# Expert steps of a mixture-of-experts trunk on one core: the down projection set directly ahead of the next up projection, the first scatter moved ahead of the gather, and the token tiles stored in the order in which they are loaded as weights

## The chip, the cores and the metric

The kernel runs on one core of a Trainium2 chip. Its time is the device time of one execution in microseconds (us); lower is better. A run gives a median over several executions. The profiled execution is one more, and its trace shows every instruction of every engine.

## The reference, cut to what matters

Two decoder layers over 256 tokens of width 1024, all in fp32. Each has an attention mixer, a layer norm, a mixture of experts, another layer norm and a gated embedding. The change lies in the mixture:

```python
s = sigmoid(xf @ router_w)                       # 64 experts, 8 groups
eidx = top_k(masked s + bias, 8)                 # 8 experts for each token
gates = s[eidx] / sum(s[eidx]) * 2.5
for each expert e, over the tokens that chose it:
    h = silu(xe @ w1[e]) * (xe @ w3[e])          # 1024 -> 256
    out[tok] += (h @ w2[e]) * gate               # 256 -> 1024
out += (silu(xf @ sw1) * (xf @ sw3)) @ sw2       # shared expert
```

## The kernel before, in words

Every expert gets 64 slots. The experts are taken in pairs: a **step** m works on two experts (128 slots), there are 32 steps in a layer, and four steps share one **octet** of eight experts. The slots' tokens aren't fetched by index; TensorE picks them with one-hot matrices that VectorE (DVE in the profile) builds.

What TensorE (PE) does in a step, in program order, with the line of the profile:

- **up** (`exp_up`, L907): 32 fp32 matmuls of 256 columns, which the trace shows as 64; the two experts use the two 64-column halves of the array (the profile's `128*64`). The tokens' slots are the weights, the expert's w1 and w3 in `ring` stream past.
- **gather** (`gather`, L877): two chunks of 128 features of the next octet's tokens, 8 fp32r matmuls of 512 columns on the whole array. x is split into `x_hi` and `x_lo`; a chunk of one of them is the weights, and the one-hot `sel` streams past. Feature chunk c is every eighth column, `part[:, t, c::8]`: neighbouring weights lie 32 bytes apart. It runs in the first 28 steps of a layer.
- **h transpose** (`h_transpose`, L917): 2 transposes of the step's hidden values; needs DVE's `gate_h` (L1673). ScalarE (ACT) copies the result to `hT`.
- **scatter 0** (`scatter`, L949): 4 fp32r matmuls that add the step before's outputs `y_hi` and `y_lo` into token tile 0, by the transposed one-hot `selT`, into PSUM banks 6 and 7.
- **down** (`exp_down`, L935): 8 fp32 matmuls of 512 columns (16 in the trace), on column halves as up is.
- **one-hot transpose** (`sel_transpose`, L889 and L892): 4 small bf16 matmuls for the next step; they write the PSUM bank that the h transpose used, so they wait for ACT's copy of it.
- **scatter 1** (L949): the same as scatter 0 for token tile 1, into the same two banks; it needs DVE to have added scatter 0 to `y_acc` (`add_y`, L1681).

DVE's step is `dve_step`: `gate_h`, in the last step of an octet the one-hots for the gather two octets ahead (`sel_build`, L1640, which waits for the octet's last gather), `add_y` for tile 0, `add_y` for tile 1, and `y_low` (L1687). ACT's step is silu, the copy of `hT`, the copy of the gathered tokens, `y_high` (L1249) and the copy of `selT`. SyncE (SP) loads weights into a ring of four experts: 4 MB of w1 and w3 for step m+2 once up of step m is done, then 2 MB of w2 once down of step m is done, each as DMAs of 1 MB. GpSimd (POOL) makes `x_lo` (L481, L482) once for each layer as soon as a tile's layer norm is written, and `x_hi` (L485) once the shared expert's up projection has read `xT`, whose memory it takes; the first gather waits for both. All orders are fixed by the code, and engines wait for each other by semaphores.

Of the kernel before, what the change touches and what calls it, by code (L numbers as in the profile page):

```python
# [6 lines left out]
ALU = mybir.AluOpType  # L7
# [6 lines left out]
P = 128  # L14
D = 1024
DC = D // P
# [94 lines left out]
def build_trunk(nc, a, out):  # L111
    with ExitStack() as ctx:
# [5 lines left out]
        def sem(name):  # L118
            if name not in sems:
                sems[name] = ctx.enter_context(nc.semaphore(name))  # L120
            return sems[name]
# [297 lines left out]
        @block.gpsimd  # L419
        def _(pool):  # L420
            pool.memset(small[:, 0:1024], 0.0).then_inc(sem("small_zero"), 1)
            pool.wait_ge(w_loaded[1], loaded[1])
            pool.dma_start(bgate[:, :], a["ev_b_gate"][0].partition_broadcast(P)).then_inc(sem("bias_loaded"), 16)
            pool.dma_start(fox_b[:, :], a["od_b_f"][0].partition_broadcast(P)).then_inc(sem("bias_loaded"), 16)
            pe_t = qkT[:, 16, 0:2 * HD]
            pool.dma_start(pe_t[0:CMP_LEN, 0:HD], a["ev_cmp_pos_k"][0]).then_inc(sem("cmp_loaded"), 16)
            pool.dma_start(pe_t[0:CMP_LEN, HD:2 * HD], a["ev_cmp_pos_v"][0]).then_inc(sem("cmp_loaded"), 16)
            pool.dma_start(cmp_w1[0:HD], a["ev_cmp_w1_k"][0].rearrange("(l d) f -> d l f", d=HD)).then_inc(sem("cmp_loaded"), 16)
            pool.dma_start(cmp_w1[HD:P], a["ev_cmp_w1_v"][0].rearrange("(l d) f -> d l f", d=HD)).then_inc(sem("cmp_loaded"), 16)
            pool.wait_ge(sem("small_zero"), 1)  # L430
            pool.dma_start(small[0:HD, 0:HD], a["ev_cmp_w2_k"][0]).then_inc(sem("cmp_loaded"), 16)
            pool.dma_start(small[0:HD, HD:2 * HD], a["ev_cmp_w2_v"][0]).then_inc(sem("cmp_loaded"), 16)
            def load_layer(L):
                if L == 0:
                    pool.wait_ge(sem("proj_mm0"), 2 * NT)
                else:

                    pool.wait_ge(sem(f"router_mm{L - 1}"), NT)
                    pool.wait_ge(sem(f"router_dve{L - 1}"), NT)
                    pool.wait_ge(sem(f"pT_tp{L - 1}"), NT)  # L440
                pool.dma_start(router_w[:, :, :], a["router_w"][L].rearrange("(p c) n -> p c n", c=DC)).then_inc(sem("layer_loaded"), 16)
                pool.dma_start(router_b[:, :], a["router_bias"][L].partition_broadcast(P)).then_inc(sem("layer_loaded"), 16)
                pool.dma_start(p_tok[:, :, :], a["p"][L, 0].rearrange("(t p) n -> p t n", p=P)).then_inc(sem("layer_loaded"), 16)
                load_rows(L, 0)

            def load_rows(L, n):

                g, b = (("ln1_g", "ln1_b"), ("ln2_g", "ln2_b"), ("ple_norm_g", "ple_norm_g"))[n]
                if 3 * L + n:

                    pool.wait_ge(sem("gb_used"), NT * (3 * L + n))
                pool.dma_start(gb_row[:, 0, :], a[g][L].partition_broadcast(P)).then_inc(sem("gb_loaded"), 16)
                pool.dma_start(gb_row[:, 1, :], a[b][L].partition_broadcast(P)).then_inc(sem("gb_loaded"), 16)

            load_layer(0)

            steps = [0]

            def step(ins):

                steps[0] += 1
                ins.then_inc(sem("pool_step"), 1)
                pool.wait_ge(sem("pool_step"), steps[0])

            pool.wait_ge(sem("const_loaded"), 16)
            for n, (src, heads, dst) in enumerate(((QB, 8, 20), (KS, 1, 28), (KW, 1, 30))):

                for t in range(NT):
                    pool.wait_ge(sem(f"proj_t{t}_0"), (4, 4, 5)[n])
                    ins = rope(pool, step, *rope_views(t, src, heads, dst), rope_tmp[:, :])  # L470
                    if t < NT - 1:
                        step(ins)
                ins.then_inc(sem("roped_nsa"), 1)
                pool.wait_ge(sem("roped_nsa"), n + 1)
            for L in range(DEPTH):
                if L:
                    load_layer(L)

                for t in range(NT):
                    pool.wait_ge(sem(f"ln1_out{L}"), t + 1)  # L480
                    step(pool.tensor_copy(x_lo[:, t, :], x_tok[:, t, :]))  # L481
                    step(pool.tensor_tensor(x_lo[:, t, :], x_tok[:, t, :], x_lo[:, t, :], ALU.subtract))  # L482
                pool.wait_ge(sem("shared_up"), NT * (L + 1))
                for t in range(NT):
                    pool.tensor_copy(x_hi[:, t, :], x_tok[:, t, :]).then_inc(sem("x_split"), 1)  # L485

                pool.wait_ge(sem("place_max"), L + 1)
                pool.partition_all_reduce(over_all, over_row, P, bass.bass_isa.ReduceOp.max).then_inc(sem("place_all"), 1)

                pool.wait_ge(sem("exp_up"), L * PAIRS + PAIRS - 4)  # L490
                load_rows(L, 1)
                load_rows(L, 2)
# [16 lines left out]
        def _(pe):  # L509
# [86 lines left out]
            for L in range(DEPTH):  # L596
# [273 lines left out]
                def gather(o, j, bank=0):  # L870

                    if j == 0:
                        pe.wait_ge(sem("sel_built"), o + (O0 + 1))
                    for c in range(2):
                        for t in range(NT):
                            for part in (x_hi, x_lo):
                                ins = pe.matmul(ps[:, bank + c, :], part[:, t, 2 * j + c::DC], sel[:, t, :],  # L877
                                                start=(t == 0 and part is x_hi), stop=(t == NT - 1 and part is x_lo))
                    ins.then_inc(sem("gathered"), 1)

# [59 lines left out]
                def scatter(m, t, par, first, bank=6):  # L940

                    if t == 0:
                        pe.wait_ge(sem("y_split"), m + (M0 + 1))
                    if bank == 6 and not (first and t == 0):

                        pe.wait_ge(sem("y_added"), 2 * m + (2 * M0 + t))
                    for half in range(2):
                        for part in (y_hi, y_lo):
                            ins = pe.matmul(ps[:, bank + half, :], selT[:, par, t * P:(t + 1) * P],  # L949
                                            part[:, half * PIECE:(half + 1) * PIECE],  # L950
                                            start=(part is y_hi), stop=(part is y_lo))
                    ins.then_inc(sem("scattered"), 1)

                def pe_step(m, o, odd, u, gather_next=True, selT_next=True, scatter_last=True, first=False):


                    par = u % 2
                    for b in range(2):
                        k = ks + 1 + 2 * par + b
                        if isinstance(m, int):  # L960
                            pe.wait_ge(w_loaded[k % RING], 32 * (m // 2) + loaded[k])
                        else:
                            pe.wait_ge(w_loaded[k % RING], 16 * (m - par) + loaded[k])
                    exp_up(m, o, odd, u, par, first and M0 == 0)
                    if gather_next:
                        pe.wait_ge(sem("xe_copied"), 4 * o + (4 * O0 + 4 + u))
                        gather(o + 1, u)
                    h_transpose(m)
                    if scatter_last:
                        scatter(m - 1, 0, 1 - par, M0 == 0 and isinstance(m, int) and m == 1)  # L970
                    exp_down(m, par, first and M0 == 0)
                    if selT_next:
                        sel_transpose(m + 1, o + 1 if u == 3 else o, (u + 1) % 4)
                    if scatter_last:
                        scatter(m - 1, 1, 1 - par, False)


                pe.wait_ge(sem("x_split"), NT * (L + 1))
# [330 lines left out]
        def _(dve):  # L1309
# [149 lines left out]
            for L in range(DEPTH):  # L1459
# [229 lines left out]

                def dve_step(m, o, u, build=True, build_bf=True, add=True):  # L1690
                    gate_h(m, u % 2)
                    if build and u == 3:
                        sel_build(o + 2)
                    if add:
                        add_y(m - 1, 0)
                        add_y(m - 1, 1)
                    y_low(m)
                    if build_bf and u == 2:
                        sel_bf_build(o + 1)
# [80 lines left out]
```

## Time and profile before

| | before |
|---|---|
| median of 3 runs (lowest, highest) | 1493.35 us (1493.33, 1494.79) |
| the profiled execution's own time | 1495.15 us |
| its span | 1493.4 us |
| PE busy | 1432.8 us, 96% |
| DVE, ACT, POOL busy | 34%, 24%, 3% |
| DMA | 461.89 MB, mean 309 GB/s |
| granted TensorE clock, mean | 0.981 |

The two stretches of expert steps are from 224 to 709 us and from 954 to 1439 us of the span. PE's busy time counts matmuls from start to end; since they are pipelined, the distance from one start to the next, and not a matmul's own duration, tells what one costs.

### The profile page before, as it was taken

How to read it: one execution, taken by the hardware profiler on the slowest of the kernel's cores; microseconds unless marked ns; L12 is line 12 of the kernel's file. 1: busy time of each engine (PE TensorE's matmuls, PEld its weight loads, DVE VectorE, ACT ScalarE, POOL GpSimd, SP SyncE). 2: the span in 40 equal slices, each digit the busy share in tenths (PEclk: the TensorE clock that was granted, in tenths of full speed). 3: DMA queues.
4: the chain of work that ended last, by engine and by line, in shares of the span. 5: the costliest groups of instructions: out<-in, count | busy, mean ns of one | idle time of the engine just before them, and what ended most of it. 6: DMA issues, size and time to landing. Idle time of an engine off the chain costs nothing.

```text
span 1493.4 us, 21684 instructions
## 1 busy us (share of the span) xinstructions
PE 1432.8 (96%) x8704; PEld 900.3 (60%) x8704; DVE 508.3 (34%) x840; ACT 356.5 (24%) x878; POOL 50.2 (3%) x75
## 2 busy tenths in 40 slices
PE   8978999999999999999899999999999999999988
PEld 3467586566565656654478476765666656565543
DVE  0397261332323223232610346222323322232253
ACT  1137132222222222221210242222222222222211
POOL 1220010000000000000100001000000000000000
PEclk9969999999999999999899999999999999999999
DMA  9530147999999999998564504499999999999951
GB/s 308 181 148 1 74 178 322 400 416 407 413 414 412 411 405 414 408 418 343 166 213 145 225 2 169 174 420 411 400 409 414 410 421 405 413 404 409 421 211 56
DMA packets 80807, 461.89 MB, mean 309 GB/s; under 512 B 9168, under 2 KB 9392, under 8 KB 30544
## 3 DMA queue, kind: packets, MB, share of 16 engines
q1 hardware_dynamic: 78128, 452.07, 75.1%
q0 software_dynamic: 2592, 8.53, 1.9%
q8 instruction: 71, 1.16, 0.3%
q14 instruction: 16, 0.13, 0.0%
HBM read 459.52 MB, written 1.05 MB: 308 GB/s over the span
## 4 chain that ended last, share of the span: by engine, by line
PE 91%; DVE 5%; ACT 2%; issue 1%; DMA 0%; SPq 0%; DVEq 0%
PE ps L907 30%; PE ps L935 15%; PE ps L877 10%; PE ps L949 9%; PE ps L1053 4%; PE ps L794 4%; PE ps L749 3%; PE ps L634 3%; PE ps L766 2%; PE ps L818 2%; PE ps L590 1%; PE ps L917 1%; PE ps L619 1%; PE ps L513 1%; PE ps L734 1%; PE ps L827 1%
## 5 line engine op out<-in xcount | busy, mean ns | idle before, releaser
L1681 DVE TENSOR_TENSOR o_tok<-ps,o_tok 128x1024 f32<-128x1024 f32 x128 | 156.6, 1224 | 347.0 <-PE ps L949 347.0
L935 PE MATMUL ps<-ring,qkT 128*64 128x512 f32 x1024 | 233.8, 598 | 1.2 <-ACT qkT L1228 1.2
L907 PE MATMUL ps<-ring,proj 128*64 128x256 f32 x2048 | 228.1, 381 | 0.0
L907 PEld LDWEIGHTS ps<-ring,proj 128*64 128x64 f32 x2048 | 144.2, 137 | 80.8 <-issue 11.5
L935 PEld LDWEIGHTS ps<-ring,qkT 128*64 128x64 f32 x1024 | 68.2, 136 | 133.3 <-issue 133.3
L1673 DVE SCALAR_TENSOR_TENSOR roped<-roped,rows,ps 128x256 f32<-128x256 f32 x64 | 30.7, 480 | 316.1 <-ACT roped L1222 316.1
L1249 ACT ACTIVATE y_hi<-ps 128x1024 fp32r<-128x1024 f32 x64 | 65.6, 1024 | 293.4 <-PE ps L949 287.4
L907 PE MATMUL ps<-ring,pT 128*64 128x256 f32 x1024 | 123.1, 382 | 2.2 <-ACT gb_row L1216 2.2
L907 PE MATMUL ps<-ring,gb_row 128*64 128x256 f32 x1024 | 121.5, 379 | 0.0
L877 PE MATMUL ps<-sel,x_hi 128*128 128x512 f32 x256 | 118.2, 462 | 0.0
L949 PE MATMUL ps<-y_hi,selT 128*128 128x512 f32 x256 | 112.5, 439 | 4.0 <-DVE y_lo L1687 4.0
L877 PE MATMUL ps<-sel,x_lo 128*128 128x512 f32 x256 | 103.9, 406 | 0.0
L1222 ACT ACTIVATE roped<-ps 128x256 f32<-128x256 f32 x64 | 24.6, 385 | 329.1 <-PE ps L907 329.1
L949 PE MATMUL ps<-y_lo,selT 128*128 128x512 f32 x256 | 102.6, 401 | 0.0
L907 PEld LDWEIGHTS ps<-ring,pT 128*64 128x64 f32 x1024 | 71.6, 137 | 44.0 <-issue 12.5
L877 PEld LDWEIGHTS ps<-sel,x_hi 128*128 128x128 f32 x256 | 83.2, 325 | 22.0 <-issue 22.0
L907 PEld LDWEIGHTS ps<-ring,gb_row 128*64 128x64 f32 x1024 | 74.5, 137 | 36.0
L877 PEld LDWEIGHTS ps<-sel,x_lo 128*128 128x128 f32 x256 | 85.4, 334 | 0.2
L1687 DVE TENSOR_TENSOR y_lo<-ps,y_hi 128x1024 fp32r<-128x1024 f32 x64 | 77.7, 1214 | 13.7 <-ACT y_hi L1249 13.7
L1053 PE MATMUL ps<-ring,xT 128*128 128x512 f32 x128 | 60.5, 634 | 2.2 <-ACT xT L1064 2.2
L794 PE MATMUL ps<-ring,xT 128*128 128x512 f32 x128 | 56.1, 594 | 2.2 <-ACT xT L1064 2.2
L949 PEld LDWEIGHTS ps<-y_hi,selT 128*128 128x128 f32 x256 | 49.4, 193 | 11.6 <-DVE y_lo L1687 4.3
(248 smaller groups left out, 1404.3 us busy)
## 6 DMA issues: line engine op xcount, KB each, us to landing
ring<-in_exp_w_dram SPq DMA_DIRECT2D x384, 1024.0 KB, 10.9
ring<-in_od_w_in_dram SPq DMA_DIRECT2D x6, 2048.0 KB, 8.5
ring<-in_ple_w_gate_dram SPq DMA_DIRECT2D x4, 2048.0 KB, 10.4
ring<-in_ev_w_in_dram SPq DMA_DIRECT2D x3, 2048.0 KB, 21.2
ring<-in_sh_w_dram SPq DMA_DIRECT2D x6, 1024.0 KB, 6.9
ring<-in_ev_w_o_dram SPq DMA_DIRECT2D x2, 2048.0 KB, 11.0
ring<-in_od_w_o_dram SPq DMA_DIRECT2D x2, 2048.0 KB, 8.4
ring<-in_ev_w_in_dram SPq DMA_DIRECT2D x2, 1024.0 KB, 9.9
```

Of the source, the lines that this page charges most:

```text
L634: ins = pe.matmul(ps[:, 4 + (2 * j + t) % 4, 0:c1 - c0], xT[:, c, t * P:(t + 1) * P], w[:, c, :], start=(c == 0), stop=(c == DC - 1))
L749: ins = pe.matmul(ps[:, (2 * j + half) % 4, b * SEQ:(b + 1) * SEQ], w[:, c, (2 * half + b) * P:(2 * half + b + 1) * P], xT[:, c, :], start ...
L794: ins = pe.matmul(ps[:, 4 + 2 * t + n, :], xT[:, c, t * P:(t + 1) * P], w[:, c, :], start=(c == 0), stop=(c == DC - 1))
L877: ins = pe.matmul(ps[:, bank + c, :], part[:, t, 2 * j + c::DC], sel[:, t, :], start=(t == 0 and part is x_hi), stop=(t == NT - 1 and part ...
L907: ins = pe.matmul(ps[b * SLOTS:(b + 1) * SLOTS, 2, w * FE:(w + 1) * FE], xe(odd, c)[:, u * P + b * SLOTS:u * P + (b + 1) * SLOTS], views[b ...
L935: ins = pe.matmul(ps[b * SLOTS:(b + 1) * SLOTS, 4 + half, :], hT[:, f, b * SLOTS:(b + 1) * SLOTS], views[b][:, f, half * PIECE:(half + 1) ...
L949: ins = pe.matmul(ps[:, bank + half, :], selT[:, par, t * P:(t + 1) * P], part[:, half * PIECE:(half + 1) * PIECE], start=(part is y_hi), ...
L1053: ins = pe.matmul(ps[:, 2 * t + n, :], xT[:, c, t * P:(t + 1) * P], w[:, c, :], start=(c == 0), stop=(c == DC - 1))
L1249: act.activation(y_hi[:, :], ps[:, 4:6, :], ACT.Copy).then_inc(sem("y_high"), 1)
L1673: dve.scalar_tensor_tensor(h_exp, h_silu, slot_gate[:, par:par + 1], ps[:, 2, FE:2 * FE], ALU.mult, ALU.mult)\
L1681: dve.tensor_tensor(y_acc[:, t, :], ps[:, bank:bank + 2, :].rearrange("p b n -> p (b n)"), y_acc[:, t, :], ALU.add)\
L1687: dve.tensor_tensor(y_lo[:, :], ps[:, 4:6, :].rearrange("p b n -> p (b n)"), y_hi[:, :], ALU.subtract)\
```

## The change

Three things. PE's step is now up, scatter 0, gather, h transpose, scatter 1, one-hot transpose, down, and the next step's up follows down. DVE adds the first scatter ahead of `sel_build`. POOL writes `x_hi` and `x_lo` in chunk order (for each token the 128 features of chunk 0, then chunk 1, ...), so that the gather loads its weights from neighbouring words; each of POOL's instructions on them reads `x_tok` in order and writes, or reads and writes, words that lie 512 bytes apart.

```diff
                 for t in range(NT):
                     pool.wait_ge(sem(f"ln1_out{L}"), t + 1)
-                    step(pool.tensor_copy(x_lo[:, t, :], x_tok[:, t, :]))
-                    step(pool.tensor_tensor(x_lo[:, t, :], x_tok[:, t, :], x_lo[:, t, :], ALU.subtract))
+                    lo = x_lo[:, t, :].rearrange("p (c n) -> p n c", c=DC)
+                    x_t = x_tok[:, t, :].rearrange("p (n c) -> p n c", c=DC)
+                    step(pool.tensor_copy(lo, x_t))
+                    step(pool.tensor_tensor(lo, x_t, lo, ALU.subtract))
                 pool.wait_ge(sem("shared_up"), NT * (L + 1))
                 for t in range(NT):
-                    pool.tensor_copy(x_hi[:, t, :], x_tok[:, t, :]).then_inc(sem("x_split"), 1)
+                    pool.tensor_copy(x_hi[:, t, :].rearrange("p (c n) -> p n c", c=DC),
+                                     x_tok[:, t, :].rearrange("p (n c) -> p n c", c=DC)).then_inc(sem("x_split"), 1)
...
                             for part in (x_hi, x_lo):
-                                ins = pe.matmul(ps[:, bank + c, :], part[:, t, 2 * j + c::DC], sel[:, t, :],
+                                ins = pe.matmul(ps[:, bank + c, :], part[:, t, (2 * j + c) * P:(2 * j + c + 1) * P], sel[:, t, :],
                                                 start=(t == 0 and part is x_hi), stop=(t == NT - 1 and part is x_lo))
...
                     exp_up(m, o, odd, u, par, first and M0 == 0)
+                    if scatter_last:
+                        scatter(m - 1, 0, 1 - par, M0 == 0 and isinstance(m, int) and m == 1)
                     if gather_next:
                         pe.wait_ge(sem("xe_copied"), 4 * o + (4 * O0 + 4 + u))
                         gather(o + 1, u)
                     h_transpose(m)
                     if scatter_last:
-                        scatter(m - 1, 0, 1 - par, M0 == 0 and isinstance(m, int) and m == 1)
-                    exp_down(m, par, first and M0 == 0)
+                        scatter(m - 1, 1, 1 - par, False)
                     if selT_next:
                         sel_transpose(m + 1, o + 1 if u == 3 else o, (u + 1) % 4)
-                    if scatter_last:
-                        scatter(m - 1, 1, 1 - par, False)
+                    exp_down(m, par, first and M0 == 0)
...
                 def dve_step(m, o, u, build=True, build_bf=True, add=True):
                     gate_h(m, u % 2)
+                    if add:
+                        add_y(m - 1, 0)
                     if build and u == 3:
                         sel_build(o + 2)
                     if add:
-                        add_y(m - 1, 0)
                         add_y(m - 1, 1)
```

PE's program in one step before, after the step's up (rows 341 and 342 are that up, 366 is the next one's; the waits are semaphores):

```order
341 L907 MATMUL ps<-ring,proj 64x256 [waits exp_h,w_loaded1,w_loaded0]
342 L907 MATMUL ps<-ring,proj 64x256 x31
343 L877 MATMUL ps<-sel,x_hi 128x512 [waits xe_copied]
...
351 L917 MATMUL ps<-const,roped 128x128 [waits selT_copied,exp_h]
353 L949 MATMUL ps<-y_hi,selT 128x512 [waits y_added,y_split]
...
357 L935 MATMUL ps<-ring,qkT 64x512 [waits hT_copied,y_split,down_loaded1,down_loaded0]
359 L889 MATMUL ps<-ident_bf,sel_bf 128x128 [waits hT_copied]
362 L949 MATMUL ps<-y_hi,selT 128x512 [waits y_added]
...
366 L907 MATMUL ps<-ring,proj 64x256 [waits exp_h,w_loaded3,w_loaded2]
```

The same step in the changed program, whose lines are numbered 3 higher:

```order
341 L910 MATMUL ps<-ring,proj 64x256 [waits exp_h,w_loaded1,w_loaded0]
342 L910 MATMUL ps<-ring,proj 64x256 x31
343 L952 MATMUL ps<-y_hi,selT 128x512 [waits y_added,y_split]
...
347 L880 MATMUL ps<-sel,x_hi 128x512 [waits xe_copied]
...
355 L920 MATMUL ps<-const,roped 128x128 [waits selT_copied,exp_h]
357 L952 MATMUL ps<-y_hi,selT 128x512 [waits y_added]
...
361 L892 MATMUL ps<-ident_bf,sel_bf 128x128 [waits hT_copied]
364 L938 MATMUL ps<-ring,qkT 64x512 [waits hT_copied,y_split,down_loaded1,down_loaded0]
366 L910 MATMUL ps<-ring,proj 64x256 [waits exp_h,w_loaded3,w_loaded2]
```

Full-array work (128x...) and column-half work (64x...) alternate four times in a step of before and twice in one of the changed program. Scatter 1 now comes one gather and one h transpose after scatter 0, and down one more scatter and the one-hot transposes after the h transpose.

DVE's program in the last step of the first octet, before:

```order
267 L1673 SCALAR_TENSOR_TENSOR roped<-roped,rows,ps 128x256 [waits hT_tp,selT_copied,exp_silu]
268 L1640 TENSOR_TENSOR sel<-roped,const 128x512 [waits gathered]
269 L1640 TENSOR_TENSOR sel<-roped,const 128x512
270 L1681 TENSOR_TENSOR o_tok<-ps,o_tok 128x1024 [waits y_added,scattered] x2
271 L1687 TENSOR_TENSOR y_lo<-ps,y_hi 128x1024 [waits y_high]
```

And in the changed program:

```order
267 L1676 SCALAR_TENSOR_TENSOR roped<-roped,rows,ps 128x256 [waits hT_tp,selT_copied,exp_silu]
268 L1684 TENSOR_TENSOR o_tok<-ps,o_tok 128x1024 [waits y_added,scattered]
269 L1643 TENSOR_TENSOR sel<-roped,const 128x512 [waits gathered]
270 L1643 TENSOR_TENSOR sel<-roped,const 128x512
271 L1684 TENSOR_TENSOR o_tok<-ps,o_tok 128x1024 [waits y_added,scattered]
272 L1690 TENSOR_TENSOR y_lo<-ps,y_hi 128x1024 [waits y_high]
```

The add of tile 0 no longer stands behind the one-hots, which wait for the gather.

## Rows read from the trace of the kernel before

**Rows 1.** The page: busy time, share of the span and instructions of PE.

```profile
PE 1432.8 (96%) x8704; PEld 900.3 (60%) x8704; DVE 508.3 (34%) x840; ACT 356.5 (24%) x878; POOL 50.2 (3%) x75
```

**Rows 2.** Busy time by stretch: us, engines, granted clock, DMA share, GB/s.

```profile
299.00:629.00 330.00, 330.00 (x2209) 201.29 (x2207) 99.62 (x106) 77.72 (x195) 0.00 (x0) 1.00 1.00 411
661.00:692.00 31.00, 29.00 (x200) 15.79 (x201) 9.18 (x9) 5.76 (x17) 0.00 (x0) 1.00 1.01 421
```

**Rows 3.** PE's timeline, one step (m = 13): start us, duration, line, what.

```profile
422.35 7.13 PE L907 MATMUL ps<-ring,proj 128*64 128x256 f32 x64
429.41 0.64 PE L877 MATMUL ps<-sel,x_hi 128*128 128x512 f32 x1
429.88 0.40 PE L877 MATMUL ps<-sel,x_lo 128*128 128x512 f32 x1
430.12 0.41 PE L877 MATMUL ps<-sel,x_hi 128*128 128x512 f32 x1
...
431.59 0.39 PE L917 MATMUL ps<-const,roped 128*128 128x128 f32 x2
431.73 0.48 PE L949 MATMUL ps<-y_hi,selT 128*128 128x512 f32 x1
432.05 0.40 PE L949 MATMUL ps<-y_lo,selT 128*128 128x512 f32 x1
432.28 0.39 PE L949 MATMUL ps<-y_hi,selT 128*128 128x512 f32 x1
...
432.84 3.65 PE L935 MATMUL ps<-ring,qkT 128*64 128x512 f32 x16
436.43 0.29 PE L889 MATMUL ps<-ident_bf,sel_bf 128*128 128x128 bf16 x2
...
436.60 0.47 PE L949 MATMUL ps<-y_hi,selT 128*128 128x512 f32 x1
...
437.70 1.08 PE L907 MATMUL ps<-ring,proj 128*64 128x256 f32 x8
```

**Rows 4.** PE's timeline in step 0, where up follows the one-hot transposes.

```profile
237.92 0.29 PE L889 MATMUL ps<-ident_bf,sel_bf 128*128 128x128 bf16 x2
...
238.16 0.65 PE L907 MATMUL ps<-ring,pT 128*64 128x256 f32 x4
```

**Rows 5.** Groups of weight loads by line: busy us, mean ns of one, idle before.

```profile
L877 PEld LDWEIGHTS ps<-sel,x_lo 128*128 128x128 f32 x256 | 85.4, 334 | 0.2
...
L949 PEld LDWEIGHTS ps<-y_hi,selT 128*128 128x128 f32 x256 | 49.4, 193 | 11.6 <-DVE y_lo L1687 4.3 <-issue 1.6
...
L513 PEld LDWEIGHTS ps<-const,x_tok 128*128 128x128 f32 x96 | 13.3, 197 | 16.1 <-DVEq L1453 7.0 <-DMA const<-in_const_dram 4.3 <-issue 2.4
```

**Rows 6.** PE's timeline in steps 28 to 31, which have no gather.

```profile
652.65 7.13 PE L907 MATMUL ps<-ring,proj 128*64 128x256 f32 x64
660.77 0.50 PE L917 MATMUL ps<-const,roped 128*128 128x128 f32 x2 [1.00 <-DVE roped L1673]
...
666.99 7.13 PE L907 MATMUL ps<-ring,proj 128*64 128x256 f32 x64
...
695.69 1.52 PE L907 MATMUL ps<-ring,proj 128*64 128x256 f32 x12
```

**Rows 7.** DVE's timeline: one-hots in step 11, an add in step 13.

```profile
401.22 1.29 DVE L1640 TENSOR_TENSOR sel<-roped,const 128x512 fp32r<-128x512 f32 x2 [1.49 <-PE ps L877]
433.03 1.22 DVE L1681 TENSOR_TENSOR o_tok<-ps,o_tok 128x1024 f32<-128x1024 f32 x1 [2.61 <-PE ps L949]
```

**Rows 8.** The last w3 of step 31, issued at 675.73: median us to landing.

```profile
ring<-in_exp_w_dram SPq DMA_DIRECT2D x1, 1024.0 KB, 16.6
```

**Rows 9.** POOL's and PE's timeline ahead of the first gather of layer 0.

```profile
192.18 1.04 POOL L481 CAST x_lo<-x_tok 128x1024 fp32r<-128x1024 f32 x1 [11.15 <-DVEq L1453]
207.71 2.02 POOL L485 CAST x_hi<-x_tok 128x1024 fp32r<-128x1024 f32 x2 [12.06 <-PE ps L818]
214.55 0.80 PE L877 MATMUL ps<-sel,x_hi 128*128 128x512 f32 x1
```

## The prediction

> **What bounds the kernel now.** I read the page's busy times first: PE is busy 96% of the span, DVE a third of it [rows 1]. Next the busy times by stretch, because two things can be full at once: in the expert steps PE is busy without a gap and the clock is granted in full (1.00, the 2.4 GHz level), and the DMA share is also 1.00, at 411 GB/s [rows 2]. Then PE's timeline of one step. From one up to the next it takes 437.70 - 422.35 = 15.35 us, and no row has a bracket for a wait [rows 3]; the list of waits shows none of PE for a weight DMA. So PE sets the pace, and the weights (six DMAs of 1 MB, 6.29 MB a step) are asked for at 6.29 / 15.35 = 410 GB/s, which is the rate seen. What the DMA could do is told by the steps at the end of the layer, where more is outstanding: 421 GB/s [rows 2], or 14.94 us a step. Any PE time taken out of the step meets that floor after 0.4 us, unless there is slack. There is: the last w3 of step 31 is issued at 675.73, lands 16.6 us later at 692.3 [rows 8], and is used at 695.69 [rows 6]: 3.4 us early, the tightest place of a layer.
>
> **The change part by part**, for a step with a gather and both scatters (steps 1 to 27 of two layers, 54 steps). Prices are distances between starts in rows 3.
>
> *The column-half stretches.* If a column takes one cycle of 2.4 GHz, up (64 x 256 columns) is 6.83 us and down (16 x 512) 3.41 us. They take 7.06 and 3.59, 0.23 and 0.18 over. A part of that is at each stretch's start and end and a part in the stream. Joined, one start and one end go; I take a third of the 0.41, **0.12 us**. Entering such a stretch from a scatter also costs: a scatter's inner distance is 0.23 us (432.05 to 432.28), its last one 0.33 (432.28 to 432.84 less 0.23), so 0.10, twice. After the change the one entry follows the one-hot transposes. Step 0 shows that: 237.92 to 238.16, 0.24 us [rows 4], against 0.17 from the same transposes to a scatter. So 0.20 becomes 0.07: **0.13 us**. That down directly followed by up costs nothing of its own isn't shown anywhere; none to 0.10 us, the price of an entry.
>
> *Leaving up.* The first gather distance is 0.47 us against 0.244 later ((431.59 - 429.88) / 7): 0.23 for the weight load that nothing hides. A scatter's first distance is 0.32 against 0.23. Before, a step pays 0.23 once and 0.09 twice. After, scatter 0 takes the place behind up, its load is shorter (193 ns against 325 to 334 [rows 5]), and the gather comes behind full-array work. I price it at 0.13, with 0.09 for scatter 1: 0.41 becomes 0.22, **0.19 us**.
>
> *Contiguous gather weights.* The gather's load takes 334 ns, the scatter's 193, both fp32r beside a stream of 512 columns [rows 5]; the distances are 0.244 and 0.23 us. With 8 matmuls I take 0.09 of the 0.11: **0.09 us**. Bounds are nothing and 0.11.
> A row of before disagrees: L513 also loads every eighth word, as plain fp32, and needs 197 ns [rows 5]. By that row the layout would bring nothing. The Trainium skill (Advanced Engine Details and Errata, SBUF Cachelines) says that reads are at full rate only when neighbouring accesses fall in one 16-byte line, which words 32 bytes apart never do. L877 agrees with it, L513 doesn't. By the rule the gather term stands; by L513 it is 0, and the step keeps 0.44 us of gain.
>
> Sum: 0.12 + 0.13 + 0.19 + 0.09 = 0.53 us a step, 54 x 0.53 = 28.6 us. Step 0 of each layer has no scatter and gains about 0.2; the 32 gather matmuls ahead of it gain 32 x 0.011 = 0.35. Together 1.1, so 29.7 us.
>
> *Steps 28 to 31 (eight in all)* take 666.99 - 652.65 = 14.34 us, with a wait of 1.00 for `gate_h` [rows 6]. Scatter 0 now covers that wait, but scatter 1 then stands directly behind: it waits until DVE has added scatter 0. Scatter 0 ends some 1.2 us after it starts, the add starts 0.12 later and takes 1.22 [rows 7]: scatter 1 starts 2.6 us after scatter 0 where PE is ready after 1.3. So 1.0 goes, 1.2 to 1.3 comes, and the joined stretches give 0.2 to 0.3 back: 14.3 to 14.4 us, no change.
>
> *In the gather steps the same wait is hidden.* Between scatter 0 and scatter 1 lie scatter 0 (1.1), the gather (1.95) and the transpose (0.15): 3.2 us, against 2.6. The cover is 0.6 us. It holds in an octet's last step only because DVE's add comes ahead of the one-hots: they can't start before the gather's end and take 1.29 us [rows 7], so in the old DVE order scatter 1 would wait some 2.5 us, once in four steps. The one-hot transposes wait for ACT's copy of `hT`; a scatter lies between, as it lay ahead of down before, without a wait [rows 3].
>
> *After step 31*, scatter 1 of step 30 no longer lies behind down, so PE waits longer for `y_low`, but ACT's `y_high`, which waits for that scatter, starts as much earlier: no change.
>
> *POOL.* Writing words 512 bytes apart is in no row of before. `x_hi` is copied from 207.71 for 2.02 us and needed at 214.55: 4.8 us of cover. `x_lo` of tile 1 runs from 192.18 to 195.65 (207.71 - 12.06 idle), 12 us of cover [rows 9]. From unchanged to four times slower it costs nothing; I take nothing.
>
> *The weights.* If the DMA keeps 421 GB/s once PE presses on it, 27 steps of 14.94 instead of 15.31 us (411 GB/s) land the last w3 of a layer 10 us earlier, at 682.3. PE would want it at 695.69 - 14.9 = 680.8. It waits 1.5 us, 3 us in two layers. The Trainium skill (DMA: Bandwidth & Descriptors, Bandwidth) puts the fabric's ceiling at 435 GB/s and a long transfer at 425; by 425 the step's floor would be 14.80 us and the wait gone. The rows show 421, so the wait stays in the sum.
>
> 29.7 - 3 = **26.7 us**. The profiled execution took 1495.15 us, so 1468.5; it is 1.8 above the median of the runs, which makes 1466.7. I say **1467 us**.
>
> **The rivals.**
> 1. *The weights take most of it.* The DMA share is 1.00 at 411 GB/s too [rows 2], so 411 may be what the loads can do while gathers run, and 421 a property of the steps without gathers. Then the landings stay where they are and PE can gain only the slack of step 31, 3.4 us a layer, 7 in all: 1486. In between (half of the 10 us is gained) it is about 1477. For it: both figures are averages with no idle time. Against: at 411 the demand itself was 410, and that the two meet by chance is unlikely. Chance 0.21, most of it in the middle.
> 2. *The layout brings nothing, or the joined stretch little*: 0.36 to 0.44 us a step, 20 to 24 us, and no wait for weights: 1470 to 1474. Chance 0.12.
> 3. *Slower: POOL's strided writes.* At a factor f, `x_lo` of tile 1 and `x_hi` take 3.5 f + 2.0 f from 192.18 on, with 22.4 us until the gather: PE starts late from f = 4.1, by 5.5 us a layer for each further 1. To lose all of 27 us and more, f must pass 6.5; f = 8 makes 1510. For it: such access is unseen here. Against: the cast handles a word a nanosecond (1024 in 1.04 us [rows 9]), which is no tuned vector rate. Chance 0.04.
> 4. *The change does nothing*, because the excess of rows 3 belongs to the matmuls and not to their neighbours: 1493. Chance 0.03; rows 4 speak against it.
>
> **How the numbers follow.** The forecast (1462 to 1472) has 0.6. With rival 2 and the most of rival 1 the range of 8 in 10 is 1461 to 1483; its low end is a gain of 0.59 us a step with no wait for weights, its high end lies two thirds of the way from 1477 to the full price of rival 1. This measurement tells about 0.2% (3 us) from no change. Faster: all but rivals 3 and 4, 0.93; same 0.03; slower 0.04.
>
> **What would show it.** PE's timeline of a middle step: 14.8 to 14.9 us from up to up; no transition between down and up; the gather's load near 193 ns and its distance near 0.23; no wait ahead of scatter 1. Steps 28 to 31: a wait of 1.2 us at a scatter for DVE's add. The DMA rate rises to 418 to 423 GB/s, and if PE has bracketed waits for a weight DMA, they are late in a layer. Wrong is the forecast if those waits come in the middle of a layer, if scatter 1 waits in gather steps, or if the first gather starts later than 7 us after `x_hi`'s copy begins.

## The result and the profile after

The changed kernel takes 1470.82 us (median of 4 runs, 1469.03 to 1473.36) against 1493.39 us before: a ratio of 0.9855, 95% interval 0.9842 to 0.9867. That is 22.6 us less, where 26.7 were worked out; the profiled execution, 1473.36 us, has a span of 1471.6.

A middle step of the changed kernel, in PE's timeline (start us, duration, line, what; to be held against [rows 3]):

```profile
414.42 7.08 PE L910 MATMUL ps<-ring,proj 128*64 128x256 f32 x64
421.43 0.50 PE L952 MATMUL ps<-y_hi,selT 128*128 128x512 f32 x1
421.76 0.40 PE L952 MATMUL ps<-y_lo,selT 128*128 128x512 f32 x1
422.00 0.40 PE L952 MATMUL ps<-y_hi,selT 128*128 128x512 f32 x1
...
422.47 0.39 PE L880 MATMUL ps<-sel,x_hi 128*128 128x512 f32 x1
422.69 0.39 PE L880 MATMUL ps<-sel,x_lo 128*128 128x512 f32 x1
...
424.32 0.39 PE L920 MATMUL ps<-const,roped 128*128 128x128 f32 x2
424.46 0.48 PE L952 MATMUL ps<-y_hi,selT 128*128 128x512 f32 x1
...
425.48 0.28 PE L892 MATMUL ps<-ident_bf,sel_bf 128*128 128x128 bf16 x2
...
425.72 3.65 PE L938 MATMUL ps<-ring,qkT 128*64 128x512 f32 x16
429.21 1.03 PE L910 MATMUL ps<-ring,proj 128*64 128x256 f32 x8
```

Up to up is 14.79 us, 0.56 less than before. Down is followed by up after 3.49 us, where it took 3.59 to the transposes; up is left after 7.01 in place of 7.06; the gather's eight matmuls take (424.32 - 422.47) / 8 = 0.231 us each, the first one too. The gather's weight load, among the groups by line:

```profile
L880 PEld LDWEIGHTS ps<-sel,x_lo 128*128 128x128 f32 x256 | 48.1, 188 | 11.4 <-issue 0.5
```

188 ns where it was 334 [rows 5]. In the middle of a layer and near its end, the busy times by stretch (the last three numbers are the granted clock, the DMA share and GB/s):

```profile
292.00:613.00 321.00, 321.00 (x2223) 195.72 (x2223) 101.69 (x106) 78.66 (x197) 0.00 (x0) 1.00 1.01 421
640.00:670.00 30.00, 25.87 (x180) 15.71 (x178) 8.30 (x8) 5.37 (x16) 0.00 (x0) 1.00 1.01 421
```

From 292 us on the rate is 421 GB/s, which before was seen only at the end [rows 2]. PE is busy throughout the first stretch, and 25.87 of 30 us in the second. What it waits for there, in the last steps (PE's timeline; compare [rows 6]):

```profile
636.66 7.13 PE L910 MATMUL ps<-ring,proj 128*64 128x256 f32 x64
...
646.22 0.50 PE L952 MATMUL ps<-y_hi,selT 128*128 128x512 f32 x1 [0.94 <-DVE o_tok L1684]
...
653.02 7.13 PE L910 MATMUL ps<-ring,proj 128*64 128x256 f32 x64 [1.86 <-issue]
...
667.93 7.13 PE L910 MATMUL ps<-ring,proj 128*64 128x256 f32 x64 [0.38 <-issue]
...
683.78 7.13 PE L910 MATMUL ps<-ring,proj 128*64 128x256 f32 x64 [1.35 <-issue]
```

The bracket says "issue", which is what the profile prints when it sees no releaser. The weights tell who it is. The last w3 of step 31 is issued at 661.75 (SyncE's timeline), and the DMA view of that issue gives its KB and the us to landing:

```profile
661.75 0.38 SPq L345 DMA_DIRECT2D ring<-in_exp_w_dram  x1
ring<-in_exp_w_dram SPq DMA_DIRECT2D x1, 1024.0 KB, 21.9
```

so it lands at 683.7, and up of step 31 starts at 683.78. The slack of 3.4 us of before [rows 8] is gone: PE waits for weights ahead of the ups of steps 29, 30 and 31, and in the second layer of step 28 too, 7.4 us in all by the profile's list of waits. PE comes to step 31 at 683.78 instead of 695.69, and in the second layer it takes 460.6 us from step 0 to step 31 instead of 471.7.

### The profile page after: what moved, and what is told of

The parts are those of the page before. It is cut to its first block, busy times and chain, and to the rows that moved or that the text cites. A ratio compares the mean times of both kernels' runs of the same rounds, so it can differ in the third digit from the quotient of the medians.

```text
span 1471.6 us, 21684 instructions
## 1 busy us (share of the span) xinstructions
PE 1401.4 (95%) x8704; PEld 884.7 (60%) x8704; DVE 516.5 (35%) x840; ACT 356.4 (24%) x878; POOL 59.6 (4%) x75
## 4 chain that ended last, share of the span: by engine, by line
PE 90%; DVE 6%; ACT 2%; issue 2%; DMA 0%; SPq 0%; DVEq 0%
PE ps L910 30%; PE ps L938 16%; PE ps L952 9%; PE ps L880 8%; PE ps L1056 4%; PE ps L797 4%; PE ps L752 3%; PE ps L637 3%; PE ps L769 2%; PE ps L821 2%; PE ps L593 1%; PE ps L622 1%; PE ps L737 1%; PE ps L516 1%; PE ps L830 1%
## 5 line engine op out<-in xcount | busy, mean ns | idle before, releaser
L910 PEld LDWEIGHTS ps<-ring,proj 128*64 128x64 f32 x2048 | 153.6, 137 | 90.4 <-issue 28.1
L880 PE MATMUL ps<-sel,x_hi 128*128 128x512 f32 x256 | 101.4, 396 | 0.0
L880 PE MATMUL ps<-sel,x_lo 128*128 128x512 f32 x256 | 100.7, 393 | 0.0
L1231 ACT ACTIVATE qkT<-ps 128x256 f32<-128x256 f32 x64 | 24.6, 384 | 164.4 <-PE ps L920 164.4
L880 PEld LDWEIGHTS ps<-sel,x_hi 128*128 128x128 f32 x256 | 48.1, 188 | 12.3 <-issue 1.2
```

What stands on the lines that cost most here:

```text
L880: ins = pe.matmul(ps[:, bank + c, :], part[:, t, (2 * j + c) * P:(2 * j + c + 1) * P], sel[:, t, :], start=(t == 0 and part is x_hi), stop ...
L910: ins = pe.matmul(ps[b * SLOTS:(b + 1) * SLOTS, 2, w * FE:(w + 1) * FE], xe(odd, c)[:, u * P + b * SLOTS:u * P + (b + 1) * SLOTS], views[b ...
```

## The experiments

Twelve kernels, in three groups (the first four below, the next four, and the last four), each group on one chip. Each ratio is to the kernel before, measured in the same group. The changed kernel's own time was taken apart from all three, so times across groups are compared with care. Where it helps, two profiled executions are compared by the time from step 0's up to step 31's, which leaves out the rest of the kernel.

**The order without the layout.** `x_hi`, `x_lo` and the gather's slices as before, the rest as changed:

```diff
-                    lo = x_lo[:, t, :].rearrange("p (c n) -> p n c", c=DC)
...
-                                ins = pe.matmul(ps[:, bank + c, :], part[:, t, (2 * j + c) * P:(2 * j + c + 1) * P], sel[:, t, :],
+                                ins = pe.matmul(ps[:, bank + c, :], part[:, t, 2 * j + c::DC], sel[:, t, :],
```

> The changed order of PE and DVE, with x_hi and x_lo as before (gather weights 32 bytes apart). Theory (the gain is switches between column halves and the full array, plus the layout): a middle step takes 14.79 + 8 x (0.244 - 0.23) = 14.89 us, so about 0.46 of the 0.57 us stay; the DMA, at 14.9 us a step, is then no longer behind PE until the last four steps. 1472 to 1475 us. Rival (the layout did most): the step takes over 15.1 us and the time is above 1481.

Measured: 1467.71 us, ratio 0.9828 (0.9801 to 0.9854), below the expected 1472 to 1475 and not to be told from the changed kernel. The step is as expected: PE's timeline of this kernel has

```profile
416.62 7.08 PE L907 MATMUL ps<-ring,proj 128*64 128x256 f32 x64
...
424.67 0.41 PE L877 MATMUL ps<-sel,x_hi 128*128 128x512 f32 x1
...
426.64 0.39 PE L917 MATMUL ps<-const,roped 128*128 128x128 f32 x2
...
684.18 6.05 PE L907 MATMUL ps<-ring,proj 128*64 128x256 f32 x54 [0.90 <-issue]
```

The gather takes 0.246 us a matmul, the step 14.91 us. Yet step 31 starts at 684.18, only 0.4 us after the changed kernel's, and 460.26 us after step 0, where the changed kernel needs 460.40: in 27 steps the layout won some 3 us and lost them again at the weights. The second layer is alike (459.67 against 460.55). The other 3.1 us between the two profiled executions lie outside the expert steps, where the two differ only in POOL's copies and in the gathers ahead of step 0; why, the runs don't show.

**The layout without the order.**

```diff
+                    lo = x_lo[:, t, :].rearrange("p (c n) -> p n c", c=DC)
...
-                                ins = pe.matmul(ps[:, bank + c, :], part[:, t, 2 * j + c::DC], sel[:, t, :],
+                                ins = pe.matmul(ps[:, bank + c, :], part[:, t, (2 * j + c) * P:(2 * j + c + 1) * P], sel[:, t, :],
```

> The order of before with x_hi and x_lo in chunk order. Theory: the gather distance falls from 0.244 to 0.23 and the exposed load behind up from 0.47 to about 0.34, so a step takes 15.35 - 0.10 - 0.13 = 15.12 us, 56 steps x 0.23 = 13 us, 1480 us; the two parts alone (this and the order alone) add up to more than the whole, since both shorten the same exposed load. Rival (order and layout are independent): 15.25 us a step, 1487.

Measured: 1480.28 us, ratio 0.9913 (0.9897 to 0.993), as the theory has it. PE's timeline:

```profile
418.35 7.13 PE L910 MATMUL ps<-ring,proj 128*64 128x256 f32 x64
425.41 0.50 PE L880 MATMUL ps<-sel,x_hi 128*128 128x512 f32 x1
425.75 0.40 PE L880 MATMUL ps<-sel,x_lo 128*128 128x512 f32 x1
...
433.48 7.13 PE L910 MATMUL ps<-ring,proj 128*64 128x256 f32 x64
```

15.13 us a step; the first gather distance behind up is 0.34 where it was 0.47. The layout alone is worth 0.22 us a step, the order alone 0.44, together 0.56: they share the gather's exposed load behind up, which either of them shortens.

**DVE's old order.** The changed kernel with `sel_build` ahead of both adds:

```diff
                     gate_h(m, u % 2)
-                    if add:
-                        add_y(m - 1, 0)
                     if build and u == 3:
                         sel_build(o + 2)
                     if add:
+                        add_y(m - 1, 0)
                         add_y(m - 1, 1)
```

> The changed kernel, but DVE builds the one-hots ahead of both adds as before. Theory: in an octet's last step scatter 1 waits for gather end, 1.29 us of one-hots and an add of 1.22 us, 2.6 us, in 12 steps: +31 us of PE time. The weights get that time to land, so the some 5 us that PE waits for them late in the two layers go: 1495 to 1500 us, slower than before. Rival (some other work covers scatter 1): at 1471.

Measured: 1501.98 us, ratio 1.005 (1.0034 to 1.0067): slower than before, and 2 us above the expected 1495 to 1500. The timeline of an octet's last step:

```profile
277.29 1.29 DVE L1643 TENSOR_TENSOR sel<-roped,const 128x512 fp32r<-128x512 f32 x2 [2.07 <-PE ps L880]
278.50 1.22 DVE L1684 TENSOR_TENSOR o_tok<-ps,o_tok 128x1024 f32<-128x1024 f32 x1
279.77 0.79 PE L952 MATMUL ps<-y_hi,selT 128*128 128x512 f32 x1 [2.29 <-DVE o_tok L1684]
280.36 0.63 PE L952 MATMUL ps<-y_lo,selT 128*128 128x512 f32 x1
```

The chain is the expected one, and a wait of 2.3 to 2.4 us stands in all 12 such steps. In six of them it has a second price, which wasn't expected: the scatter behind it runs at 0.43 us a matmul in place of 0.23, while the granted clock is at 0.50. The busy times by stretch:

```profile
276.00:279.00 3.00, 1.48 (x8) 1.08 (x6) 1.71 (x3) 1.30 (x2) 0.00 (x0) 1.00 1.01 423
280.00:283.00 3.00, 3.00 (x12) 1.66 (x14) 1.12 (x1) 0.00 (x0) 0.00 (x0) 0.50 1.04 431
```

In the other six the same wait leaves the clock as it was (the matmul in PE's timeline, and the stretch behind it):

```profile
406.62 0.50 PE L952 MATMUL ps<-y_hi,selT 128*128 128x512 f32 x1 [2.42 <-DVE o_tok L1684]
```

```profile
406.62:410.00 3.38, 3.38 (x18) 1.67 (x20) 1.23 (x1) 0.00 (x0) 0.00 (x0) 1.00 1.02 427
```

Such a step takes 17.5 us, one with the lower clock 18.7 to 19.2; the six of them cost some 9 us in all. What decides between them, the runs don't show.

**The rows of the layer norm, later.** POOL loads two 0.5 MB broadcasts when up of step 27 is done; here, when up of step 30 is done (and below, step 31):

```diff
-                pool.wait_ge(sem("exp_up"), L * PAIRS + PAIRS - 4)
+                pool.wait_ge(sem("exp_up"), L * PAIRS + PAIRS - 1)
```

> The changed kernel, with the rows of the next layer norm (two DMAs of 0.5 MB from the POOL queue) loaded after the up of step 31 instead of step 27. Theory (from step 28 on PE waits for weights, which these rows push back by 2.5 us a layer): PE reaches step 31 2.5 us earlier in each layer, 1466 us; landings are 14.9 us apart in step 27 to 28 instead of 17.5. Rival (the 17.5 is something of the end of the loop): no change, 1471.

Measured: 1469.02 us, ratio 0.9836 (0.9816 to 0.9855), not clearly different from the changed kernel; the count of the semaphore made it the up of step 30 and not of step 31 as the expectation says, while step 31's weights were still due. The wait didn't go but gathered in one place. In layer 0 the granted clock fell behind it (PE's timeline and the stretches):

```profile
683.20 7.04 PE L910 MATMUL ps<-ring,proj 128*64 128x256 f32 x48 [3.28 <-issue]
```

```profile
683.00:686.60 3.60, 3.40 (x16) 2.16 (x18) 0.00 (x0) 0.00 (x0) 0.00 (x0) 0.53 1.01 411
```

In layer 1 the one wait is 2.03 us and the clock stays at 1.00.

**Fewer weights.** To take the DMA away as a bound, three quarters of each w3 load are left out from the fifth expert on, so those experts compute with an older w3:

```diff
+                sp.dma_start(ring[:, slot, UP_N:UP_N + 512], w3.rearrange(rows_of, c=DC)[:, 0:512]).then_inc(w_loaded[slot], 16)
```

In the kernel before:

> The kernel before, with three quarters of each w3 load left out from the fifth expert on (so the result of those experts is computed with an older w3; 4.7 MB a step are loaded instead of 6.3). Theory (before, PE never waits for weights): steps stay at 15.35 us and the time at 1493. Rival (the rate of the loads slows PE's own operands): steps get shorter than 15.3.

Measured: 1494.12 us, ratio 1.0014 (1.0005 to 1.0023); steps at 15.35 us. Before, the weights bound nothing.

In the changed kernel:

> The changed kernel with the same loads left out. Theory (weights are the floor only from step 28 on): steps with a gather stay at 14.79 us, steps 28 to 31 take 14.28, PE reaches step 31 some 4.6 us earlier in a layer: 1462 us. Rival (the lost microseconds are the clock or the end of the layer): 1470.

Measured: 1461.63 us, ratio 0.9795 (0.9778 to 0.9811). The last steps in PE's timeline, now without a bracket:

```profile
637.01 7.08 PE L914 MATMUL ps<-ring,proj 128*64 128x256 f32 x64
651.29 7.08 PE L914 MATMUL ps<-ring,proj 128*64 128x256 f32 x64
```

A step without gather takes 14.28 us, and the kernel 9.2 us less than the changed one. The steps show the same: from step 0 to step 31 it takes 455.87 us in both layers, where the changed kernel takes 460.40 and 460.55, 9.2 us more. That is the price of the weights.

In the order without the layout:

> The changed order without the layout, with the same loads left out. Theory (with full loads the layout's 0.12 us a step are given back to the DMA floor): steps stay at 14.91 us, so this is 54 x 0.12 = 6.5 us slower than the changed kernel with the same loads, 1468 us, while with full loads the two can't be told apart. Rival (the layout is worth nothing in the new order): equal to it.

Measured: 1468.01 us, ratio 0.9842 (0.9826 to 0.9859). Without the DMA's bound the layout is worth 6.4 us; with it, nothing that the runs can tell.

**The rows after the last up.**

```diff
-                pool.wait_ge(sem("exp_up"), L * PAIRS + PAIRS - 4)
+                pool.wait_ge(sem("exp_up"), L * PAIRS + PAIRS)
```

> The changed kernel with the rows of the next layer norm loaded after the up of step 31. With the wait after step 30's up, they still stood ahead of nothing but met the last w3 on the engines, and the wait moved to step 31. Theory: now they meet no expert weights of w1 and w3, PE reaches step 31 some 2.5 us earlier than in the changed kernel in each layer, 1466 us. Rival (the layer norm waits for the rows instead): 1471.

Measured in five runs: 1466.26 us (1465.94 to 1468.13), ratio 0.9831 (0.9817 to 0.9845). Of three waits for weights in the last steps of layer 0 one of 1.48 us is left, and step 31 starts at 682.11. From step 0 to step 31 it takes 457.70 and 458.13 us, 5.1 less in two layers than the changed kernel: the rows' 1 MB a layer is over half of the 9.2. It has the lowest median of the kernels here with the whole computation, 4.6 us under the changed one, but the two were measured apart, their intervals overlap a little, and the order alone (1467.71) isn't told apart from it either.

**Down and up apart again.** The one-hot transposes behind down:

```diff
-                    if selT_next:
-                        sel_transpose(m + 1, o + 1 if u == 3 else o, (u + 1) % 4)
                     exp_down(m, par, first and M0 == 0)
+                    if selT_next:
+                        sel_transpose(m + 1, o + 1 if u == 3 else o, (u + 1) % 4)
```

> The changed kernel with the one-hot transposes moved behind down again, so that down and the next up no longer touch; all else as changed. Theory: leaving down for the full array costs 0.10 us and entering up from the transposes 0.24 in place of the 0.24 ahead of down, now 0.33 from the scatter; together 0.2 to 0.3 us a step, 15.0 to 15.1 us a step, the DMA no longer behind PE, 1476 to 1480 us. Rival (the gain came from scatter 0 behind up and the layout, and adjacency of down and up is worth nothing): steps at 14.8 us, 1471.

Measured: 1474.8 us, ratio 0.9877 (0.9855 to 0.9899), 1 us under the expected range. PE's timeline:

```profile
418.40 7.13 PE L910 MATMUL ps<-ring,proj 128*64 128x256 f32 x64
...
429.57 3.65 PE L938 MATMUL ps<-ring,qkT 128*64 128x512 f32 x16
433.16 0.28 PE L892 MATMUL ps<-ident_bf,sel_bf 128*128 128x128 bf16 x2
433.28 0.20 PE L895 MATMUL ps<-gates_bf,sel_bf 128*128 128x6 bf16 x2
433.40 0.87 PE L910 MATMUL ps<-ring,proj 128*64 128x256 f32 x6
```

A step takes 15.01 us in most places (15.00 in this one) and PE doesn't wait for weights: the adjacency is worth 0.22 us, the rest of the order about as much again. In time it is only 4 us, since the changed kernel gives part of its gain to the weights.

**The distance of the weights.** `x_hi` and `x_lo` with k = 2 or 4 chunks interleaved, so that the gather's neighbouring weights lie 8 or 16 bytes apart (4 in the changed kernel, 32 before):

```diff
-                    lo = x_lo[:, t, :].rearrange("p (c n) -> p n c", c=DC)
-                    x_t = x_tok[:, t, :].rearrange("p (n c) -> p n c", c=DC)
+                    lo = x_lo[:, t, :].rearrange("p (a n b) -> p n a b", b=4, n=P)
+                    x_t = x_tok[:, t, :].rearrange("p (n a b) -> p n a b", b=4, n=P)
```

> The changed kernel with the gather's weights 8 bytes apart (chunks in pairs, interleaved). Theory (two words of each 16 bytes are used): the load stays near 188 ns and the gather distance at 0.23 us, step 14.79. Rival (anything but neighbours is slow): load above 250 ns.

> The changed kernel with the gather's weights 16 bytes apart (chunks in fours, interleaved). Theory (one word of each 16 bytes is used, as at 32 bytes apart): the load takes 325 to 335 ns, the gather distance 0.244 us, step 14.91. Rival (it is the 32 bytes): load near 190 ns.

Measured, one execution each: 1471.95 us for 8 bytes, 1471.11 us for 16. The weight loads, at 8 and at 16 bytes (groups by line):

```profile
L880 PEld LDWEIGHTS ps<-sel,x_lo 128*128 128x128 f32 x256 | 49.5, 193 | 10.2 <-issue 0.5
```

```profile
L880 PEld LDWEIGHTS ps<-sel,x_lo 128*128 128x128 f32 x256 | 79.2, 309 | 0.2
```

The theory is right on the load: it jumps between 8 and 16 bytes. It is wrong on the price: at 16 bytes the gather distance is 0.235 us ((425.03 - 423.15) / 8 in that kernel's timeline) and the step 14.81 us. A load of 309 ns is all but hidden (0.004 us a matmul over the changed kernel's 0.231), one of 330 ns costs 0.015 (0.246 in the order without the layout).

**The order, with late rows.** The first and the fourth edit (waiting for step 31) together:

> The changed order without the layout, with the rows of the next layer norm loaded after the up of step 31. Theory (the DMA's 14.9 us a step is the floor with or without the layout): PE comes to step 31 at the same time as with the layout and the late rows, 1466 to 1468 us. Rival (the layout still counts): 6 us more, 1472.

Measured in five runs: 1470.8 us (1468.03 to 1471.98), ratio 0.9844 (0.9828 to 0.986), nearer to the rival. Here PE has no wait for weights left, and step 31 starts at 683.62, 1.5 us later than with the layout. So once the rows are out of the way, the DMA doesn't cover the slower step any more. From step 0 to step 31 it takes 459.07 and 459.08 us, 2.3 more than with the layout and the late rows. The medians of the two, from different chips, are 4.5 us apart; the part outside these steps isn't settled: the clock falls at other places behind the last step in each execution (0.88 against 0.99 between 698 and 712 us).

## Why the prediction was right, point by point

- **The joined stretches**, 0.12 us: 3.49 + 7.01 us against 3.59 + 7.06, 0.15. The prediction called its 0.12 a third of 0.41, which is 0.14.
- **Entering them**, 0.13 us: transposes to down take 0.24 us (425.48 to 425.72), as step 0 had shown for up [rows 4]. The scatters in all take 1.04 and 1.02 us where they took 1.11 and 1.10; with the 0.07 back for the transposes and 0.01 that belongs to the next point, 0.09. The joined stretches and the entry together: moving the transposes back costs 0.22 us a step.
- **Leaving up**, 0.19 us: behind up the first scatter distance is 0.33, a penalty of 0.10 where I took 0.13. With 0.09 for scatter 1, and nothing left of the gather's 0.23, 0.41 becomes 0.19: 0.22.
- **The layout**, 0.09 us: 8 x (0.244 - 0.231) = 0.10. The 8 and 16 byte kernels bear out the Trainium skill's rule on 16-byte lines (Advanced Engine Details and Errata, SBUF Cachelines) for this load: 193 ns with two words in a line, 309 with one. That L513's load keeps 197 ns at 32 bytes stays unexplained. The term holds in the step; in the time it was lost to the weights (the order alone is as fast).
- **The sum**: 0.53 us a step predicted, 0.56 to 0.57 measured (0.15 + 0.09 + 0.22 + 0.10). With light weights the kernel before and the changed one differ by 1494.12 - 1461.63 = 32.5 us, where I had 29.7 before the DMA.
- **Steps 28 to 31**: the wait moved from `gate_h` to DVE's add (0.95 us, 1.2 forecast), and with light weights the step takes 14.28 where 14.3 to 14.4 were expected. With full weights it takes 14.9 to 16.4, which the prediction put down to the weights and sized too small (below).
- **The cover of scatter 1** held in gather steps, and only by DVE's new order: with the old one the same kernel is slower than before.
- **POOL**: the casts take 1.9 times as long (`x_hi` 3.78 us for two against 2.02), within the factor 4.1 that the cover allows; the first gather starts at 214.33, against 214.55 [rows 9].
- **The weights**: right in kind and place, too small in size. The predicted wait was 1.5 us a layer, 3 in all; the steps of the light kernel put it at 9.2. The step of the working that failed is "27 steps of 14.94 instead of 15.31 us (411 GB/s) land the last w3 of a layer 10 us earlier, at 682.3". It landed at 683.7, 8.6 us earlier: in the changed kernel's trace the w3 of most steps land 14.9 us apart, those of a few 15.4 to 15.9, and those of steps 28 and 29, where the rows are loaded too, 16.0 and 16.4. And PE, with 0.57 us a step, would have been there near 679.3 (step 0 at 223.38, plus the light kernel's 455.87) and not at 680.8.
- **What that did to the time**: step 31 starts when its weights have landed, so what PE gained beyond the forecast only made the wait longer. The landing, 1.4 us late in each layer, is some 3 of the 4 us by which the time is above 1467. Over half of the wait was the rows', a term that the prediction took over from before inside the 3.4 us of slack and didn't price: behind the last up they give 5.1 us back.
- **The rivals**: rival 1 at full price is out, since the weights came at 421 GB/s in the steps with gathers too; 411 was the demand, not the limit. The time lies where rival 2 had it, 1470 to 1474, but not for its reason: the step kept 0.56 us of gain, and PE did wait for weights.

Without the weights' term PE's gain came out 2.8 us above the forecast, with it the time 4 us above it, inside the range. That the weights land every 14.9 us was measured; why single steps took longer was not tried.

## What to carry to other kernels

When PE and the DMA are both full, work out the time per step of each before pricing a PE saving; here the floor lay 0.45 us under a step, and one of two savings was lost to it. Count the other loads on the same DMA engines as well: 1 MB of rows near the end cost 2.4 to 2.7 us a layer. The distance between starts in PE's timeline, at each change of tile shape, priced the four parts of this reordering to 0.04 us each before it was made. And an operation that is moved needs its partner on the other engine moved too: without DVE's reordering the same PE order takes 31 us more.

## What the runs showed of the hardware

- Some PE waits of 2.3 us and more inside dense work were followed by a granted clock near 0.50, the lower level, for about 3.4 us: six of the 12 waits of 2.3 to 2.4 us with DVE's old order (280 to 283 us, where the scatter ran at 0.43 us a matmul), and the one of 3.28 us with the rows after step 30 (0.53 from 683 to 686.6). The other six left it at 1.00 (406.62 to 410), and so did waits of 0.9 to 1.9 us in the changed kernel (640 to 670) and one of 2.03 us.
- The weight load of 128 x 128 fp32r took 188, 193, 309 and 330 ns at 4, 8, 16 and 32 bytes between words; beside a 512-column stream the pace was 0.231, 0.232, 0.235 and 0.246 us, so only the last one showed much.
- Copying on POOL with destination words 512 bytes apart took 1.9 to 2.0 us for 128 x 1024 instead of 1.04, and the subtraction 2.88 instead of 2.35.
